# Where ScalarE splits two weights, drains four query tiles, and where VectorE turns the key, in a two-layer attention stage

## The reference

```python
h = x @ w_in
(a_q, a_k, a_v, a_z, b_cq, b_ckv, b_kr, b_z, c_q, c_k, c_v, c_z) = jnp.split(h, _split_points(), axis=-1)
ya = moba_attention(...) * silu(a_z)
cq = _rmsnorm(b_cq, gq)
ckv = _rmsnorm(b_ckv, gkv)
qh = _split_heads(cq @ w_uq, MLA_HEADS)
q_b = concat([qh[..., :64], _rope(qh[..., 64:], pos)])
kvh = _split_heads(ckv @ w_ukv, MLA_HEADS)
k_b = concat([kvh[..., :64], broadcast(_rope(b_kr[:, None], pos))])
yb = mla_attention(q_b, k_b, kvh[..., 64:]) * silu(b_z)
yc = diff_attention(...) * silu(c_z)
```

## Time and profile before

| | us |
|---|---|
| median of 3 runs | 2122.8 |
| lowest and highest | 2121.53, 2125.31 |
| the profiled execution | 2122.98 |
| its span, first to last instruction | 2121.2 |
| PE busy | 2082.5 |
| DVE busy | 1398.6 |
| ACT busy | 1298.9 |
| POOL busy | 676.4 |

### The profile page before, as it was taken

How to read it: one execution, slowest core, us unless ns; L and a number is a source line. 1 busy time by engine, 2 the same in 40 slices (tenths; PEclk the granted TensorE clock), 3 DMA queues, 4 the chain that set the end, 5 groups by cost and what they waited for, 6 DMA issues and landing times.

```text
span 2121.2 us, 33729 instructions
## 1 busy us (share of the span) xinstructions
PE 2082.5 (98%) x13391; PEld 1868.4 (88%) x13395; DVE 1398.6 (66%) x1428; ACT 1298.9 (61%) x1452; POOL 676.4 (32%) x335
## 2 busy tenths in 40 slices
PE   9989999998999999999999999999999999999998
PEld 8979999988999898999998888888888888888887
DVE  1544323344413794323787999999999999999997
ACT  4556545455644544444545777777777777777776
POOL 5646885845788303988201000000000000000000
PEclk9989999999999999999999999999999999999999
DMA  7434554633455434666447999999999999999995
GB/s 245 132 104 139 179 197 152 194 97 118 160 198 180 124 117 140 200 198 192 145 140 246 385 374 334 375 357 370 358 351 365 356 374 350 363 354 373 367 365 205
DMA packets 308658, 529.07 MB, mean 249 GB/s; under 512 B 13890, under 2 KB 153314, under 8 KB 308544
## 3 DMA queue, kind: packets, MB, share of 16 engines
q1 hardware_dynamic: 307520, 525.92, 71.3%
q0 software_dynamic: 736, 1.00, 0.2%
q10 hardware_dynamic: 288, 0.52, 0.1%
HBM read 525.84 MB, written 1.05 MB: 248 GB/s over the span
## 4 chain that ended last, share of the span: by engine, by line
PE 89%; ACT 3%; DVE 3%; POOL 2%; DMA 1%; issue 1%; SPq 0%; ACTq 0%; DVEq 0%; POOLq 0%
PE bank L776 87%; POOL weights_low L3234 2%; PE bank L1641 1%; ACT sc L1786 1%; ACT weights_high L1789 1%; DVE sc L2497 1%; DMA ring<-in_w_in_dram 0%; PE bank L1037 0%; DVE cq L2497 0%; DMA ring<-in_mla_w_uq_dram 0%; DMA ring<-in_w_ple_dram 0%; DVE nmax L2524 0%; DVE sc L2489 0%; DVE h L2497 0%; PE bank L787 0%
## 5 line engine op out<-in xcount | busy, mean ns | idle before, releaser
L2489 DVE TENSOR_TENSOR expert_weights_low<-ring_experts,expert_weights_high 128x2048 fp32r<-128x2048 f32 x336 | 764.8, 2289 | 72.5 <-ACT expert_weights_high L1789 72.4
L1789 ACT ACTIVATE expert_weights_high<-ring_experts 128x2048 fp32r<-128x2048 f32 x336 | 647.4, 1927 | 165.7 <-PE bank L776 161.4
L3234 POOL TENSOR_TENSOR weights_low<-ring,weights_high 128x1024 fp32r<-128x1024 f32 x252 | 616.8, 2470 | 280.4 <-ACT weights_high L1789 168.9
L1789 ACT ACTIVATE weights_high<-ring 128x1024 fp32r<-128x1024 f32 x294 | 304.0, 1057 | 327.7 <-PE bank L776 288.0
L776 PE MATMUL bank<-x_high,weights_high 128*128 128x256 f32 x1024 | 230.1, 281 | 5.0 <-POOL weights_low L3234 4.8
L776 PE MATMUL bank<-x_high,weights_low 128*128 128x256 f32 x1024 | 226.8, 278 | 0.0
L776 PEld LDWEIGHTS bank<-x_high,weights_high 128*128 128x128 f32 x1024 | 184.2, 189 | 7.9 <-issue 6.4
L776 PEld LDWEIGHTS bank<-x_high,weights_low 128*128 128x128 f32 x1024 | 184.1, 189 | 0.5 <-issue 0.5
L776 PE MATMUL bank<-expert_weights_high,gathered_high 128*128 128x512 f32 x456 | 180.7, 396 | 0.3 <-DVE gathered_low L2497 0.3
L776 PE MATMUL bank<-expert_weights_high,gathered_low 128*128 128x512 f32 x456 | 177.8, 390 | 0.0
L776 PE MATMUL bank<-expert_weights_high,gathered_high_b 128*128 128x512 f32 x448 | 177.5, 396 | 0.0
(11 more groups left out here) (380 smaller groups left out, 3780.3 us busy)
## 6 DMA issues: line engine op xcount, KB each, us to landing
ring_experts<-in_moe_w_gate_dram SPq DMA_DIRECT2D x112, 1024.0 KB, 7.0
ring_experts<-in_moe_w_up_dram SPq DMA_DIRECT2D x112, 1024.0 KB, 6.8
ring_experts<-in_moe_w_down_dram SPq DMA_DIRECT2D x112, 1024.0 KB, 6.5
ring<-in_w_in_dram SPq DMA_DIRECT2D x62, 1024.0 KB, 5.3
ring<-in_w_merge_dram SPq DMA_DIRECT2D x24, 1024.0 KB, 5.1
ring<-in_w_out_dram SPq DMA_DIRECT2D x14, 1024.0 KB, 5.2
ring<-in_ffn_w_gate_dram SPq DMA_DIRECT2D x11, 1024.0 KB, 5.3
ring<-in_ffn_w_up_dram SPq DMA_DIRECT2D x11, 1024.0 KB, 5.4
```

Of the source, the lines that this page charges most:

```text
L1789: return nc.scalar.activation(dst, src, ACT.Copy, scale=scale)
L2489: return nc.vector.tensor_tensor(dst, x, z, op)
L3234: nc.gpsimd.tensor_tensor(half_of(wlo[:, q_slot, :], t, width), half_of(ring[:, slot, :], t, width), half_of(whi[:, q_slot, :], t, width). ...
```

## The change

Four edits, the same in both layers:

- The transfers: the first query weight and az0's weight go ahead of the two plain weights of mc2; the second query weight follows them. `USED1` lists the weights in the order in which PE turns to them, which stays what it was.
- ACT: `latent_high(0)` goes ahead of `after("mc0")`; `latent_high(1)` and `(2)` go behind the key's copy; `after("mc1")` goes ahead of the drains of un0 to ur1, and these go ahead of `exps(3)`.
- DVE: the key's rotation and the first half of the values' copy go into softmax 3, between the maxima and the reciprocals.
- POOL: the first latent weight's low part is made behind mc1's low part, the other three behind az0's, as before.

```diff
-    + [("w_in", 2048, 256, 8), ("w_in", 2304, 256, 8), ("w_in", 2560, 128, 8), ("w_in", 2688, 32, 8), ("w_in", 1536, 256, 8)]
-    + [("w_uq", c, 384, 3) for c in (0, 384)] + [("w_ukv", c, 512, 2) for c in (0, 512)]
+    + [("w_in", 2048, 256, 8), ("w_in", 2304, 256, 8), ("w_uq", 0, 384, 3), ("w_in", 1536, 256, 8)]
+    + [("w_in", 2560, 128, 8), ("w_in", 2688, 32, 8), ("w_uq", 384, 384, 3)] + [("w_ukv", c, 512, 2) for c in (0, 512)]
...
-TAKEN1 = [list(range(len(UNITS1[0]))), [1, 2, 0] + list(range(3, len(UNITS1[1])))]
+LATER1 = [("w_in", 1536, 256, 8), ("w_uq", 0, 384, 3)]
+USED1 = [x for x in PLE_UNITS + REST1 if x not in LATER1]
+_at = USED1.index(("w_uq", 384, 384, 3))
+USED1[_at:_at] = LATER1
+TAKEN1 = [[units.index(x) for x in USED1] for units in UNITS1]
...
                 take_y(1)
+                latent_high(0)
                 after("mc0")
                 latent(0)
                 exps(2)
...
-                latent_high(0)
-                latent_high(1)
                 take_turned(2)
                 b = G1.wait_full(act, layer, "ms")
                 inv_std(rstd[:, 0:2, :], views(b), 1, dr_a.h, drained_at(layer, "ms")).then_inc(std_done.h, 1)
                 b = G1.wait_full(act, layer, "r4")
                 copy(kr[:, :], views(b)[:, 0, :]).then_inc(dr_a.h, 1)
+                latent_high(1)
+                latent_high(2)
                 gate_tanh("az0", 0)
-                latent_high(2)
                 take_y(2)
                 latent_high(3)
-                exps(3)
+                after("mc1")
                 for j in range(2):
                     drain(layer, f"un{j}", qb[:, 2 * j:2 * j + 2, :], MLA_D ** -0.5)
                     b = G1.wait_full(act, layer, f"ur{j}")
                     act.mul(qb[:, 4 + j, :], views(b)[:, 0, :], MLA_D ** -0.5).then_inc(dr_a.h, 1)
+                exps(3)
                 for j in range(2):
                     drain(layer, f"kn{j}", kb[:, 2 * j:2 * j + 2, :])
-                after("mc1")
...
-                def softmax(n):
+                def softmax(n, between=None):
...
                         sc_max.h, 1)
+                    if between:
+                        between()
                     dve.wait_ge(p_exp.h, p_exp.at(layer, n + 1))
...
-                softmax(3)
...
-                rope("rk", kr[:, :].unsqueeze(1), 0).then_inc(roped.h, 1)
...
-                values(0)
+                def key_and_values():
+                    rope("rk", kr[:, :].unsqueeze(1), 0).then_inc(roped.h, 1)
+                    values(0)
+
+                softmax(3, key_and_values)
...
-                    if q == SPLIT1.index("az0"):
-                        for i in range(LATENT1):
+                    if SPLIT1.index("mc1") <= q <= SPLIT1.index("az0"):
+                        for i in range(1) if q == SPLIT1.index("mc1") else range(1, LATENT1):
                             pool.wait_ge(lat_hi.h, lat_hi.at(layer, i + 1))
```

## The result

| | before | changed |
|---|---|---|
| median, us | 2122.16 | 2094.79 |
| lowest and highest, us | 2121.03, 2125.31 | 2093.92, 2095.48 |
| runs | 4 | 4 |
| the profiled execution, us | 2122.98 | 2093.92 |
| its span, us | 2121.2 | 2092.0 |

The changed kernel is faster: the ratio of the times is 0.9868, with a 95% interval of 0.9851 to 0.9886. That is 27.4 us by the medians and 29.1 us by the two profiled executions. The forecast of 2095.0 us was right to 0.2 us.

A forecast was written before the change was run, and what follows sets the result against it. PE bounds the kernel, busy 98% of the span, so only its idle time and low clock can go. Idle 20.3 + clock 8.4 = 28.7, taken as 28.0: 2122.98 - 28.0 = 2095.0 us, range 2092 to 2105.

The forecast's parts named there:

- Step 1: First query weight split on ACT after take_y(1), its transfer issued two units earlier, az0's one earlier; counted as 0.
- step 2: Second query weight moved behind turned probabilities, deviation and key's copy; PE's waits for pT and y (0.9, 1.9 us, first layer) go.
- Step 3: az1's split ahead of the query drains on ACT: PE's 2.3 us wait for POOL goes, with 2.2 us margin at rk.
- Rival A: az1's transfer lands over 2.2 us late, rk waits again, 1 to 3 us a layer: 2099 to 2105, chance 0.13.
- Step 4: Query drains before exponentials 3 on ACT: PE's wait before rk, 3.9 us first layer, goes; margin 1.2 us at mv1.
- Step 5: Key turned and first values copied within softmax 3 on DVE: hidden; probabilities ready near 141.5, PE turns them at 146.9.
- rival B: DVE and POOL block each other: 0 to 1.5 us a layer, 2095 to 2098, up to 2101; worse half's chance 0.12.
- The clock term: Low-clock windows behind PE's waits go to full clock: 6.4 us in the first layer, 2.0 in the second, together 8.4.
- Rival C: Each drained bank has another late waiter, so the 14 us come back before bz0: 2119 to 2124, chance 0.04.
- rival D: Slower: the key's 32 columns land too late for PE, a loss of 5 to 10 us: 2128 to 2133, chance 0.03.

The follow-up runs named there:

- the key split alone: Changed kernel with only the key's first product and the values' copy within softmax 3, the other two products behind the probabilities: 2092.45 us, ratio 0.9865.
- with y first: The key split alone, plus y3's copy ahead of cz0's split on ACT: 2090.24 us, ratio 0.9857; again beside the changed kernel (2095.34 us), 2092.12 us.
- edit 1 undone: Changed kernel with the old order of transfers and first query weight split behind mc2's drain, its low part behind az0's: 2103.2 us, ratio 0.9911.
- edit 5 undone: Changed kernel with the key's rotation and the first values' copy behind softmax 3 again: 2111.36 us, ratio 0.9947.

## Why the prediction was right, point by point

**What bounds the kernel:** right. The gain lies to 28.6 of 29.1 us in the two stretches named. The waits that went are those of the earlier trace rows, less the 0.7 a layer that came.

**Step 1, "I count 0":** wrong as the worth of the edit, right as a term of the sum. PE gains nothing where the first query weight is split (its 0.3 us before turning 2 did go, and az0 began no earlier for it). But without it the second weight's transfer comes later, ACT stands 3.2 us for it, and the kernel loses 8.4 us. The prediction had the mechanism in step 2 ("its slot is now freed by az0's low half") and entered its whole worth there.

**Step 2:** right. No wait for `pT` is listed any more and none of the longer kind for `y`; the second query weight was there at 118.03.

**Step 3:** the mechanism was right, the margin mis-sized. The landing was worked out for 129.3. It was seen at 129.03, but in an execution that ran 1.35 us ahead at that point, so it came 1.1 us late. POOL's part is 0.9 of that: the second query weight's low parts took 2.02 + 2.04 instead of the 1.82 + 1.33 taken from the earlier trace rows, since DVE was splitting the latents beside them (one subtraction of that split rose from 0.96 to 2.49). PE came 0.7 us earlier than worked out, because values 2 and the unbroken scores 3 took 3.0 us and not the 3.65 of the rows, in which a wait stood among them. So the margin at rk was not 2.2 but 0.5 us (un0 drained at 131.5, rk at 132.07). Rival A stayed off, but by a quarter of the distance that I had given it.

**Step 4:** right. kn0 was drained at 136.6 and mv1 begun at 137.15; that margin was 0.5 instead of 1.2.

**Step 5:** right in kind, but wrong by the prediction's own sign ("if PE waits for DVE before turning 3"), and here the largest error lies. The probabilities were to be ready at 141.5 with PE wanting them at 146.9, a margin of 5.4 us. They came at 145.2, which is 146.6 on the scale of the kernel before, so 5.1 us late. Of that, 0.7 lie in the key's products and 4.4 in scaling and adds. PE was ready 1.0 us early. 5.4 - 5.1 - 1.0 = -0.7, the wait that is seen in each layer. This is rival B, within its window of 145 to 148, in the milder half of its 0 to 1.5 us a layer. The forecast had counted that half in its own range but took 0 for it in the sum. The price that the rows gave, 2.2 us for a scaling, was met almost to the digit (4.03 - 1.82 = 2.21). The adds paid too, 2.1 us here and up to 4.3 in other runs. The rival had them in its "two or three of the four probability steps", though none of the rows shows a lengthened add; the nearest in the trace of before is the query's last product, which took 2.73 us at 152.23, beside POOL, where the one before it took 0.68.

**The clock term:** nearly right, with a term missing beside it. PE's busy time in the two stretches fell by 6.8 and 3.0 us, together 9.9 unrounded, where the prediction had 7.7 (6.4 and 2.0, less 0.7 for what doesn't follow the clock). The parts from un0 on, where the low windows lie, gave 8.1 of it, so the windows were counted well. The reduction was fair, if not for the reason given: weight loads do follow the clock for the most part (329 ns at the low level, 188 at the upper one), but in the low window behind rk a matmul starts every 0.213 us (nine from 487.03 to 488.95) and in the changed kernel every 0.118, a ratio of 1.8 and not of 2. The missing term is the 1.7 us of busy time that waits had cost at a granted clock of 1.00, 0.87 in each layer between az0 and un0. The sum put it at nothing, as it took a wait for its idle time alone. In the second layer the mean clock over the whole stretch, 0.92, would have said 3.4 us, too much, because part of its low clock fell on idle time.

**Why the number was so near:** the two stretches were to give 28.0, made of 20.3 of idle time and 7.7 of clock once everything is taken off, and gave 28.6, made of 18.7 of idle time, 8.1 of low clock and 1.7 of the missing term. The 1.6 less of idle time, 1.4 of which is DVE's wait, and the 2.2 more of busy time nearly cancel. That is luck. So is part of the rest: the two profiled executions differ by 29.1, of which 1.35 arose before 52 us, and the forecast started from one of them, while the median of the changed kernel lies 0.9 above its profiled execution. The bound "nothing lies below 2094 but noise" was wrong: the key split alone went to 2092.45, and with y first to 2090.24 and 2092.12, by ending the waits of 0.7 and 0.25 us a layer. Rival C and rival D left no sign; PE has no wait at the key's 32 columns.

## What to carry to other kernels

When an engine takes its list in order, look for the one instruction that waits for a transfer and ask who is queued behind it: here one line moved behind the few short operations that had queued up behind it gave half of the gain. When a step is moved beside another engine's work, take the durations of every SBUF-to-SBUF operation from a row in which that other engine was busy, since here two adds cost 1.15, 3.23 or up to 5.45 us by their company alone. Don't count a wait as its idle time alone when it falls within a group of short matmuls: 0.25 us cost 0.85 here. And keep only what frees the bank inside the critical stretch; the rest of a rotation can follow.

## What the runs showed of the hardware

- **A wait of one length is not always answered in the same way.** Behind PE's 1.87 us wait for `y` before 129.91 the first layer of the kernel before has 0.57 of the clock from 131 to 135. In its second layer the same wait, before 473.03 and of 1.87 us too, is followed by 1.00 up to 482. With the matmuls of zeros added further down, the same wait, at 129.68 with 1.87 us, is followed by a window from 131 to 135 at 1.00, as the row below shows. With edit 1 undone, 1.83 us before 459.51 were followed by 6 us at 0.50. So waits of 1.5 to 1.9 us are now and then paid twice over, and what decides it these runs don't show. Scatter between executions is no sign of it: 5.9 us with edit 1 undone and 8.6 in ten runs with the zeros, but also 5.6 for the first four of the key split with y first, which has no such wait.

```profile
131.00:135.00 4.00, 4.00 (x38) 4.00 (x37) 3.93 (x8) 0.00 (x0) 2.18 (x2) 1.00 0.63 180
```

- **DVE's price beside POOL falls on whole instructions.** An operation on two SBUF inputs of 0.41 us took 2.50 where a POOL subtraction was under way, and two of 0.57 each took 5.33 and 5.45 together where the first met one at its start: with edit 5 undone 2.72 and 2.58 us, each ended by the end of one of POOL's two pieces. With a bank as an input DVE was not lengthened beside POOL: 0.42 for the product at 132.70, 0.68 for the copy at 149.16, under POOL's pieces of 131.70 and 148.65.

- **A wait within a group of short matmuls costs more than it lasts.** Sixteen matmuls of scores take 1.61 us unbroken; broken behind the twelfth they take 2.21 us besides a wait of 1.87, and 2.21 besides one of 0.25, at a granted clock of 1.00 in each case.
